# Transposes of the identity that nobody reads, among the modulation products and in the context steps of attention

## What is computed

```python
def trunk_layer(x, mod, lw, ctx, pos):
    m = lambda i: mod[:, i][:, None, :]
    h = rmsnorm(x, ng[0]) * (1.0 + m(1)) + m(0)
    x = x + 0.5 * m(2) * rmsnorm(swiglu(h, ...), ng[1])
    h = rmsnorm(x, ng[2]) * (1.0 + m(4)) + m(3)
    mixed, ctx_out = token_mixer(h, lw, ctx, pos)
    x = x + m(5) * rmsnorm(mixed, ng[3])
    ...
mod = (silu(c) @ w_mod[l] + b_mod[l]).reshape(-1, 9, D_MODEL)      # c_ctx for the context tokens

def attend(q, k, v, scale):        # context tokens attend to context tokens only
    s = einsum('bqhd,bkhd->bhqk', q, k) * scale
    return einsum('bhqk,bkhd->bqhd', softmax(s), v)
```

## Time and profile before

| | |
|---|---|
| runs | 3040.98, 3043.66 and 3054.54 us, median 3043.66 |
| the profiled execution | 3037.54 us, of it a span of 3035.7 |
| mean granted TensorE clock in it | 0.981 of full speed |
| PE busy | 2909.6 us (96% of the span), 26152 instructions |
| DVE busy | 2166.3 us (71%) |
| ACT busy | 1297.3 us (43%) |
| POOL busy | 421.4 us (14%) |

### The profile page before, as it was taken

One profiled execution on the slowest core, in us unless ns is written; L12 is line 12 of the kernel. 1 busy time (PEld: TensorE's weight loads), 2 busy tenths in 40 slices (PEclk: granted clock), 3 DMA queues, 4 the chain that ended last, 5 costly groups with the idle time before them and its releaser, 6 DMA issues.

```text
span 3035.7 us, 62428 instructions
## 1 busy us (share of the span) xinstructions
PE 2909.6 (96%) x26152; PEld 2602.1 (86%) x26152; DVE 2166.3 (71%) x3229; ACT 1297.3 (43%) x2179; POOL 421.4 (14%) x471
## 2 busy tenths in 40 slices
PE   6999999999988899999999999999998889999998
PEld 5999878996777689998799998799877777999986
DVE  4987686756766788876878776867667767787635
ACT  3135444235543441453532554532454435345434
POOL 1000111002334320001100001110033333000100
PEclk8999999999999999999999999999998989999999
DMA  6522444410000244125452225453010004322234
GB/s 252 201 70 84 153 153 153 165 60 27 30 5 14 101 172 167 70 70 183 150 194 87 94 70 198 147 177 129 20 52 7 3 14 161 112 70 84 84 125 173
DMA packets 92916, 325.10 MB, mean 107 GB/s; under 512 B 10288, under 2 KB 13936, under 8 KB 77296
## 3 DMA queue, kind: packets, MB, share of 16 engines
q1 hardware_dynamic: 92656, 321.39, 30.0%
HBM read 318.05 MB, written 3.31 MB: 106 GB/s over the span
## 4 chain that ended last, share of the span: by engine, by line
PE 82%; DVE 11%; issue 3%; ACT 2%; DMA 2%; POOL 0%; SPq 0%; ACTq 0%; DVEq 0%; POOLq 0%
PE PS L2612 22%; PE PS L2678 20%; PE PS L2727 19%; PE PS L2622 3%; PE PS L814 2%; PE PS L1589 2%; PE PS L838 1%; DMA wo<-in_wo 1%; PE PS L1568 1%; PE PS L761 1%; PE PS L1581 1%; DVE wo_lo L3147 1%; ACT wo_hi L2846 1%; PE PS L826 1%; DVE part_lo L3207 1%
## 5 line engine op out<-in xcount | busy, mean ns | idle before, releaser
L2612 PE MATMUL PS<-h_hi,wi_hi 128*128 128x384 f32 (+2 forms) x1632 | 407.4, 312 | 10.9 <-issue 10.9
L2612 PE MATMUL PS<-h_hi,wi_lo 128*128 128x384 f32 (+2 forms) x1632 | 404.3, 310 | 0.0
L2612 PE MATMUL PS<-h_lo,wi_hi 128*128 128x384 f32 (+2 forms) x1632 | 404.1, 310 | 0.0
L2727 PE MATMUL PS<-wo_hi,a_hi 128*128 128x512 f32 x968 | 391.0, 404 | 13.1 <-DVE wo_lo L3147 9.9
L3147 DVE TENSOR_TENSOR wo_lo<-wo,wo_hi 128x1024 fp32r<-128x1024 f32 x208 | 255.5, 1228 | 194.0 <-ACT wo_hi L2846 193.1
L2727 PE MATMUL PS<-wo_hi,a_lo 128*128 128x512 f32 x968 | 378.4, 391 | 0.0
L2727 PE MATMUL PS<-wo_lo,a_hi 128*128 128x512 f32 x968 | 378.0, 391 | 0.0
L2846 ACT ACTIVATE wo_hi<-wo 128x1024 fp32r<-128x1024 f32 x208 | 220.2, 1059 | 302.4 <-PE PS L2727 208.9
L3207 DVE TENSOR_TENSOR part_lo<-wi,part_hi 128x512 fp32r<-128x512 f32 x378 | 255.7, 690 | 105.0 <-ACT part_hi L2888 102.0
L2888 ACT ACTIVATE part_hi<-wi 128x512 fp32r<-128x512 f32 x378 | 236.1, 630 | 190.6 <-PE PS L2678 118.7
L2612 PEld LDWEIGHTS PS<-h_hi,wi_hi 128*128 128x128 f32 (+1 forms) x1632 | 262.7, 188 | 15.1 <-issue 13.1
(11 more groups left out here) (377 smaller groups left out, 5821.5 us busy)
## 6 DMA issues: line engine op xcount, KB each, us to landing
wi<-in_wi SPq DMA_DIRECT2D x88, 1024.0 KB, 4.8
wo<-in_wo SPq DMA_DIRECT2D x176, 512.0 KB, 3.2
wm_in<-in_wm SPq DMA_DIRECT2D x104, 512.0 KB, 3.6
wi<-in_win SPq DMA_DIRECT2D x24, 1024.0 KB, 5.2
wo<-in_wout SPq DMA_DIRECT2D x32, 512.0 KB, 3.3
wm_out<-in_wm SPq DMA_DIRECT2D x24, 512.0 KB, 4.3
wm<-in_wm SPq DMA_DIRECT2D x4, 2048.0 KB, 17.4
wq<-in_wq SPq DMA_DIRECT2D x2, 1024.0 KB, 4.7
```

The lines of the kernel that those rows point to most:

```text
L2612: mm = pe.matmul(PSF[0:cols, at:at + GW[g]], st, h[:, k, GA[g]:GA[g] + GW[g]], start=(k == 0 and q == 0), stop=(k == KD - 1 and q == 2))
L2727: mm = pe.matmul(PS[:, OUT_BANK[t] + half, :], a, w[:, (V0(n) + b) % 2, kk, :], start=(u == 0 and kk == 0 and q == 0), stop=True, skip_gro ...
```

## The change

It adds instructions on TensorE and one wait, and swaps two waits. Each added instruction is `pe.transpose` of the 128x128 identity `ident` by itself, into PSUM that is overwritten before anybody reads it.

- Twelve go into bank 6 ahead of `mod_rows(3)`, behind a new wait for `s_me` to reach 3, that is until VectorE has taken the third unit's columns out of that bank.
- Eighteen go into bank 6 behind the third tile's transposes, ahead of the first FFN product.
- Three go into bank 4 at the head of `turn` in each context step (8 steps in each of 2 layers, 48 in all), and there the wait for `pt` now stands ahead of the one for `p_exp`, with the three between them.

```diff
             def turn(x_):
                 t = x_ // H_MLA
+                until(pe, l, "pt", x_)
+                if t == NL:
+                    for _ in range(3):
+                        pe.transpose(PP(4, 0, P), ident[:], ident[:])
                 until(pe, l, "p_exp", x_ + 1)
-                until(pe, l, "pt", x_)
                 if t < NL:
...
             for M in range(MOD_FIRST - 1):
                 mod_rows(M)
                 mod_columns(M)
+            pe.wait_ge(s_me, 3)
+            for _ in range(12):
+                pe.transpose(PS[:, 6, 0:P], ident[:], ident[:])
             mod_rows(3)
             transposes(0, 0)
             mod_columns(3)
             transposes(0, 1)
             transposes(0, 2)
+            for _ in range(18):
+                pe.transpose(PS[:, 6, 0:P], ident[:], ident[:])
             for n in SUBN:
```

## The result

The changed kernel takes 3050.79 us (median of 20 runs, 3043.43 to 3055.79) against 3043.31 us before (20 runs, 3037.21 to 3054.54). The ratio is 1.0025, with a 95% interval of 1.0018 to 1.0032: 7.6 us slower, between 5.5 and 9.7. A second measurement, among the experiments, gave 1.0024 (1.0015 to 1.0034). The forecast of 3047.6 us (+5.3 us from 3042.3) had the direction, and its range holds the time; the size is 2 us short, and +5.3 lies just under the 5.5 at which the interval begins.

A forecast was written before the change was run, and what follows sets the result against it. PE, busy for 96% of the span and 82% of the chain, was taken to bound the kernel. The terms +2.1 (twelve), 0 (eighteen) and +3.2 (context steps) gave +5.3 us on 3042.3: 3047.6 us, range 3038 to 3058.

The forecast's parts named there:

- transposes don't keep a clock up: Rival: at the start the clock rises only after the fourth unit's rows, transposes only delay; +7.7 us, 3050.0; chance 0.20.
- The context steps, +3.2: Attention's context steps: transposes in steps 32 to 35 on the chain, 36 to 39 free; 1.6 us per layer, +3.2 both.
- the sign: Context steps, profile after: distance from step 33's transpose of `Pm` to step 34's would be 1.6 us instead of 1.26.
- The twelve, +2.1: Start, ahead of the fourth unit's rows: uncovered transposes and wait, gross +2.8 us; taken as +2.1, bounds +1.4 and +4.5.
- the lower bound: Start, cost of the twelve transposes: not below +1.4 us, because PE has no idle time there to cover them.
- 1.4 us given back by the clock: Start, fourth unit's rows: if the clock still rises at 34 us, they run at full clock and return 1.4 us.
- The eighteen, 0: Ahead of the first FFN product: covered by PE's 5.74 us wait, cost 0; clock expected down as before, no gain.
- The clock stays up: Rival: at the start and in both layers, 8.3 us back against 4.0 us of costs; 3038.0; chance 0.12.
- Cover is larger: Rival: VectorE or ScalarE is as late as PE in steps 32 to 35, so 3.2 us vanish; 3044.4; chance 0.11.
- Slower: Rival: context steps keep the clock at half from 812 to 843 us without a break; +23.7 us, 3066; chance 0.05.

The follow-up runs named there:

- ctx3: Kernel before plus only the three transposes in each context step with the swapped waits, none at the start: ratio 1.0016 (1.0005 to 1.0027).
- only12: Kernel before plus only the twelve transposes ahead of the fourth unit's rows, with their wait: ratio 1.0007 (0.9999 to 1.0016).
- start30: Kernel before plus only the two edits at the start, thirty transposes and their wait, none in the context steps: ratio 1.0000 (0.9988 to 1.0012).
- late3: Kernel before plus three transposes in context steps 36 to 39 alone, waits swapped as in the change: ratio 0.9996 (0.9987 to 1.0005).
- ctx6: Kernel before plus six transposes in each context step instead of the change's three, none at the start: ratio 1.0013 (1.0003 to 1.0022).
- gap20m: Kernel before plus twenty fp32 128x128 matmuls by the identity ahead of the first FFN product: ratio 0.9997 (0.9988 to 1.0005).
- only18: Kernel before plus only the eighteen transposes ahead of the first FFN product: ratio 0.9995 (0.9986 to 1.0004).
- swap: Kernel before with only the two waits at the head of each context step swapped, no transposes: ratio 1.0000 (0.9990 to 1.0011).
- full: The whole changed kernel measured once more against the kernel before: ratio 1.0024 (1.0015 to 1.0034).
- gap40: Kernel before plus forty transposes of the identity ahead of the first FFN product, nothing else: ratio 0.9989 (0.9980 to 0.9998).
- early3: Kernel before plus three transposes in context steps 32 to 35 alone, waits swapped as in the change: ratio 1.0008 (1.0000 to 1.0017).

## Why the prediction was right, and where it was not

**Direction and range: right, by the mechanism it named.** Instructions on a PE that is busy for 96% of the time are paid where no other wait covers them. The sum was 2 us short, and the rival "transposes don't keep a clock up" had 3050.0 us, nearer to the 3050.79 measured than the forecast's 3047.6. The nearness is no proof of it: its 4.5 us for the twelve were seen in no trace.

**The context steps, +3.2: right in the trace.** 1.56 us a layer was read where 1.6 was summed. Its parts were off and cancelled: step 32 and the head of step 33 cost 0.70 and 0.38 instead of 0.64 and 0.33, and about 0.15 of step 34's was hidden, by my reading in the wait for `p_exp`, so that the distance of two steps was 1.44 us and not the 1.6 I had named as the sign. Steps 36 to 39 cost nothing, as said. The runs of ctx3 give +4.9 with an interval that holds 3.2.

**The twelve, +2.1: the mean was right, the reasoning was not.** only12 gives +2.1. But I wrote that PE has no idle time there that could cover them, because the trace before showed the fourth unit's rows starting right behind the third's columns. The weights had landed only just before. The prediction read the start off one execution and never asked when they land: in eight of the fourteen traces, all those in which the clock came up before or during the third unit's rows except start30, PE waited for them until 31.09 to 31.31 us, and the rows before started at 31.30. The waits were 0.71 to 0.88 us in four of them (changed kernel, only12, ctx3, late3) and 3.01 to 3.37 in the others (ctx6, gap20m, only18, swap). So the lower bound should have been near 0. The other term, 1.4 us given back by the clock, did not show where it was reckoned: in full, the trace whose clock is like that of the profile before, the rows still ran at half clock and the delay was 3.1 us whole. That the middle of the two bounds met the +2.1 of only12 (-0.3 to +4.9) is luck.

Here is that wait in gap20m, which has no twelve:

```profile
27.00 1.05 PE L2583 MATMUL PS<-fold,mrow 128*128 128x2 f32 x8 [0.81 <-DVE mrow L3083]
31.24 3.64 PE L2575 MATMUL PS<-wm,cwide 128*32 128x512 f32 x16 [3.19 <-DMA wm<-in_wm]
```

**The eighteen, 0: right within the interval.** only18 is -1.5 and its interval holds 0. I expected no gain because a wait of 2.60 us elsewhere had been followed by a fall. Three of four traces show the fall, though late, so that the products were at half clock for 2.8 us in only18 and in the changed kernel's trace (5.5 in full, 5.3 before); the fourth, start30, shows none. A gain in some executions was left out of the sum.

**The rivals.** "The clock stays up" is a real mechanism, and stronger than the change's own numbers show: gap40 has it with forty transposes, start30 with eighteen, and the twelve of steps 36 to 39 put a fall off. In the change it returned less than the path cost. "Transposes don't keep a clock up", to which I gave 0.20, is refuted by gap40 for a clock that is up. What it said of the rise, that it waits for the fourth unit's rows and the twelve are only delay, is how full's trace looks (a rise just before 38 us), but the clock rose as late in early3 (37.6), which has no twelve, so it isn't shown to be their doing. "Cover is larger" holds for the twelve in some executions, not for the context steps. The rival "Slower", a clock at half without a break through the steps, was seen in none of the traces.

**What stays open.** The sum was +5.3, the measurement +7.6 (5.5 to 9.7) and +7.3 (4.6 to 10.3). The parts measured alone add up to +4.9, each with an interval of 3 to 4 us to either side. So some 2 us may be a cost that only the whole has, or chance. The traces alone would give 3.1 us for the context steps and 0 to about 3 for the twelve, by the clock of the execution. Longer stretches at half clock in the mixer behind the steps could be the rest. From 860 to 1085 us and from 2360 to 2600 together, the four traces with transposes in all context steps have 51 to 77 us at half clock, the seven without any there 41 to 60: higher, but the two overlap. The mean clock of ctx3's runs (0.9778 against 0.9789) points the same way; that of the changed kernel (0.9797) and of full (0.9793 against 0.9798) hardly does.

## What to carry to other kernels

Filler for TensorE's clock belongs inside a wait that another engine sets, with as little of the wait left over as possible: forty transposes ahead of the first FFN product, with 1.38 us left, held the clock in both of their traces (ratio 0.9989), eighteen with 3.78 us left in one of four. Three at the head of each attention step stood in front of the step's own transpose and were paid almost in full wherever PE was the one waited for. Before an instruction is called uncovered, ask when the data of the next one landed: one trace shows an engine just behind a transfer, the next shows it waiting, and a bound read off a single execution is too narrow by that.

## What the runs showed of the hardware that I had not expected

The same program's start runs in different ways: the sixteen products of a modulation unit took 1.92 or 3.64 us, by whether the clock was up, and the first FFN product of one and the same program started at 46.30 or at 49.51 us. A clock that is up early gained nothing at the start: in swap, whose start is that of the kernel before, PE then waited 3.37 us for weights, and the product started at 46.30 instead of 45.82. And transposes of a 128x128 fp32 tile, alone on PE between 40.27 and 44.8 us and followed by 1.38 us of waiting, left the granted clock at 1.00, while twelve of them, 28.09 to 30.45 us in the changed kernel's trace, did not stop it from falling.
